# Sparse attention on one core: fp32r score parts, an unrolled unit sequence with the next group's preparation in it, and modulation sums split over two engines

## The reference, cut to what matters

```
mod  = silu(c) @ w_mod + b_mod            # 2048 x 12288 weights, 100 MB
hmix = modulate(rms_norm(x), sh_a, sc_a)
proj = hmix @ w_in                        # columns for pooling, linear and sparse attention
x1   = x  + g_a * (concat(pool, gla, nsa) @ w_out)
y    = x1 + g_f * swiglu(modulate(rms_norm(x1), sh_f, sc_f))
```

```
q, k_slc, k_win: rms-normalised per head, times a gain
for each group g, each token t:
  s_c = q . k_cmp (31 compressed blocks)  - slope * distance -> softmax p_c -> o_c = p_c @ v_cmp
  s_s = q . k_slc (causal)                - slope * distance -> softmax     -> o_s
  s_w = q . k_win (causal, 512 window)    - slope * distance -> softmax     -> o_w
  o   = gate0 * o_c + gate1 * o_s + gate2 * o_w
```

## Time and profile before

| | us |
|---|---|
| median of 3 runs | 2662.19 (2658.03 to 2663.2) |
| span of the profiled execution (first to last instruction) | 2663.0 |
| PE / PEld busy | 2525.8 / 2041.4 |
| DVE / ACT / POOL busy | 898.4 / 789.2 / 997.9 |
| attention stage | about 679 to 959 of the span |

### The profile page before, as it was taken

How to read it: one execution, slowest core, us unless ns; L and a number is a source line. 1 busy time by engine, 2 the same in 40 slices (tenths; PEclk the granted TensorE clock), 3 DMA queues, 4 the chain that set the end, 5 groups by cost and what they waited for, 6 DMA issues and landing times.

```text
span 2663.0 us, 33971 instructions
## 1 busy us (share of the span) xinstructions
PE 2525.8 (95%) x11449; PEld 2041.4 (77%) x11449; DVE 898.4 (34%) x1487; ACT 789.2 (30%) x1490; POOL 997.9 (37%) x764
## 2 busy tenths in 40 slices
PE   4589999998799999989999999999999999999999
PEld 3577777876677777868888888888888888888887
DVE  4755332147666666676202020202010101010112
ACT  2023224231455542232222222222222222222221
POOL 0024334443200024435444444444444444444443
PEclk8579999998888899989999999999999999999999
DMA  8742122346311246645222222222222222222223
GB/s 305 252 135 80 64 95 81 111 160 235 107 64 63 79 153 210 224 154 184 95 95 95 95 91 91 94 95 95 95 95 94 91 92 93 95 95 95 95 94 111
DMA packets 86204, 315.74 MB, mean 119 GB/s; under 512 B 9584, under 2 KB 10240, under 8 KB 84736
## 3 DMA queue, kind: packets, MB, share of 16 engines
q1 hardware_dynamic: 84240, 303.31, 34.5%
q10 hardware_dynamic: 1904, 11.62, 1.2%
HBM read 310.69 MB, written 4.19 MB: 118 GB/s over the span
## 4 chain that ended last, share of the span: by engine, by line
PE 57%; issue 30%; POOL 10%; DVE 1%; POOLq 0%; ACT 0%; DMA 0%; DVEq 0%; ACTq 0%; SPq 0%
PE ps L363 54%; POOL wlo L315 10%; PE ps L669 1%; PE ps L640 1%; PE ps L658 1%; DVE macc L1108 0%; PE ps L647 0%; POOLq L314 0%; DMA modw<-in_mstream 0%; DVE biasT L1383 0%; PE ps L675 0%; ACT pbuf L986 0%; PE ps L625 0%; POOL kn L337 0%; DVE sbuf L1431 0%
## 5 line engine op out<-in xcount | busy, mean ns | idle before, releaser
L315 POOL TENSOR_TENSOR wlo<-raw,whi 128x512 fp32r<-128x512 f32 x728 | 960.3, 1320 | 1506.7 <-ACT whi L797 1227.3
L797 ACT ACTIVATE whi<-raw 128x512 fp32r<-128x512 f32 x612 | 386.6, 632 | 1242.8 <-PE ps L363 1237.2
L363 PE MATMUL ps<-hfH,whi 128*128 128x512 f32 x1408 | 560.1, 398 | 12.3 <-DVE hfL L1489 11.5
L363 PE MATMUL ps<-hfL,whi 128*128 128x512 f32 x1408 | 559.0, 397 | 0.0
L363 PE MATMUL ps<-hfH,wlo 128*128 128x512 f32 x1408 | 559.0, 397 | 0.0
L363 PEld LDWEIGHTS ps<-hfH,whi 128*128 128x128 f32 x1408 | 266.2, 189 | 76.2 <-issue 12.3
L363 PEld LDWEIGHTS ps<-hfH,wlo 128*128 128x128 f32 x1408 | 266.2, 189 | 62.3
L363 PEld LDWEIGHTS ps<-hfL,whi 128*128 128x128 f32 x1408 | 266.4, 189 | 61.6
L1517 DVE SCALAR_TENSOR_TENSOR x1T<-ps,modc,x1T 128x512 f32<-128x512 f32 x176 | 132.2, 751 | 456.3 <-PE ps L363 456.3
L363 PE MATMUL ps<-huH,whi 128*128 128x512 f32 x704 | 279.2, 397 | 0.5 <-DVE huL L1500 0.5
L363 PE MATMUL ps<-huH,wlo 128*128 128x512 f32 x704 | 279.1, 396 | 0.0
(11 more groups left out here) (242 smaller groups left out, 2709.3 us busy)
## 6 DMA issues: line engine op xcount, KB each, us to landing
raw<-in_wstream SPq DMA_DIRECT2D x370, 512.0 KB, 3.4
modw<-in_mstream SPq DMA_DIRECT2D x192, 512.0 KB, 4.6
xT<-in_xt SPq DMA_DIRECT2D x4, 1024.0 KB, 8.5
w1s<-in_w ACTq DMA_DIRECT2D x2, 2048.0 KB, 8.3
x1T<-in_xt ACTq DMA_DIRECT2D x4, 1024.0 KB, 8.6
out_y<-x1T SPq DMA_DIRECT2D x16, 256.0 KB, 2.0
cmpb<-in_cmp_tab ACTq DMA_DIRECT2D x1, 1024.0 KB, 7.3
ptab<-in_tabs ACTq DMA_DIRECT2D x1, 768.0 KB, 4.4
```

Of the source, the lines that this page charges most:

```text
L315: nc.gpsimd.tensor_tensor(wlo[:, s, :], raw[:, r, :], whi[:, s, :].bitcast(F32), ALU.subtract).then_inc(unit_ready, 1)
L363: ins = nc.tensor.matmul(acc, lhs, rhs, start=first and n == 0, stop=last and n == 2)
L797: A(whi[:, k % SPLIT, :], raw[:, k % 8, :], ACT.Copy).then_inc(unit_hi, 1)
```

## The change

Scores. The group's queries are laid out once for each head with both halves of the partitions the same (`qn` now holds each query twice), and after the transposes ACT writes the fp32r high part of all 128 partitions while DVE overwrites partitions 64 to 127 with the low part: `qs` holds [q_high; q_low]. Keys: `kA` holds [k_high; k_high], `kB` holds [k_low; 0]. Scores are two fp32r matmuls, qs x kA and qs x kB, in place of one fp32 matmul. The compressed scores do the same with `kcA`, `kcB`. Score banks: two instead of three, so the scores of unit n wait for the minimum of unit n-2; the third bank takes the preparation.

Unrolling. The 128 units of all groups are one straight sequence. The preparation of group g+1 is six steps (keys of two branches, queries of four tiles), done after units 9, 12, 15, 18, 21 and 24 of group g: PE transposes, ACT copies the high part, and DVE subtracts one unit later. The bias tables of the next group are made at units 26 to 31, each after the last use of the row. The combine of tile 3 stands at unit 2 of the next group.

Queries of groups 2 and 3. Their squares are summed at units 3 and 5 of group 0, ACT takes the root at unit 14, DVE the inverse at 15, and POOL multiplies.

Modulation, q 12 to 15. DVE takes the even blocks of rows into `macc` at units 8, 11, ... 29, and POOL the odd ones into `macc2` with a multiply and an add; a piece's slot is free when both are done with it. PE sums both at unit 6 of the next group. Ahead of the output stage's weight pieces SP now waits until DVE has done all 32.

In the diff `scores` is PE's, `odd_rows` and the list behind it POOL's, `prep_high` ACT's (behind the saving of the unit); the rest is DVE's.

```diff
-                    nc.tensor.matmul(ps[:, n % 3, 0:w], qT[:, r // 2, t * P:(t + 1) * P],
-                                     kz[:, 2 * b + r % 2, 0:w], start=True, stop=True).then_inc(s_psum, 1)
+                q_ = qs[g % 2][:, t, r * P:(r + 1) * P]
+                nc.tensor.matmul(ps[:, n % 2, 0:w], q_, kA[g % 2][:, b, 0:w], start=True, stop=False)
+                nc.tensor.matmul(ps[:, n % 2, 0:w], q_, kB[g % 2][:, b, 0:w], start=False,
+                                 stop=True).then_inc(s_psum, 1)
...
+            def odd_rows(q):
+                pool.wait_ge(mod_summed, q)
+                for d in range(8):
+                    pool.wait_ge(mod_landed[d % 4], 32 * q + 16 * (d // 4 + 1))
+                    src = modw[:, d % 4, U:2 * U]
+                    scal = cact[:, 2 * d + 1:2 * d + 2].to_broadcast([P, U])
+                    if d == 0:
+                        TT(macc2[:, :], src, scal, ALU.mult).then_inc(mod_used, 1)
+                    else:
+                        own(TT(src, src, scal, ALU.mult))
+                        TT(macc2[:, :], macc2[:, :], src, ALU.add).then_inc(mod_used, 1)
+                    pool.wait_ge(mod_used, 8 * q + d + 1)
...
+            gains(1)
+            odd_rows(12)
+            pool.wait_ge(rq_ready, 1)
...
+            TT(q_j, q_j, rq[:, 1, :].unsqueeze(2).to_broadcast([P, 2 * T * R, DH]), ALU.mult).then_inc(qk_norm, 1)
+            pool.wait_ge(qk_norm, 3)
+            gains(2)
+            odd_rows(13)
+            gains(3)
+            odd_rows(14)
+            odd_rows(15)
...
+            def prep_high(g, step):
+                act.wait_ge(n_tr, 6 * g + step + 1)
...
+                dst = kA[g % 2][:, step, :] if step < 2 else qs[g % 2][:, step - 2, :]
+                A(dst, ps[:, prep_bank(g, step), :], ACT.Copy).then_inc(n_hi, 1)
...
+            def prep_low(g, step):
...
+                dve.wait_ge(n_hi, 6 * g + step + 1)
+                if step < 2:
+                    V.tensor_tensor(kB[g % 2][0:64, step, :], ps[0:64, bank, :],
+                                    kA[g % 2][0:64, step, :].bitcast(F32), ALU.subtract).then_inc(n_lo, 1)
...
+            def even_rows(q, d):
...
+                dve.wait_ge(mod_landed[d % 4], 32 * q + 16 * (d // 4 + 1))
...
+                    dve.wait_ge(mod_even, 8 * q + d)
+                    ins = V.scalar_tensor_tensor(out=macc[:, :], in0=src, scalar=scal, in1=macc[:, :],
+                                                 op0=ALU.mult, op1=ALU.add)
+                ins.then_inc(mod_even, 1)
...
+                if n % 8 == 2 and n >= 8:
+                    combine(T * g + t - 1)
+                if g + 1 < G and m >= 26 and (b == 0 or r == R - 1):
+                    dve.wait_ge(s_saved, n + b)
+                    bias(g + 1, r - 1 + b)
+                if g and m == MOD_SUM_AT + 1:
+                    finish_mod(g + 11, 2)
+                if g + 1 < G and m - 1 in PREP_AT:
+                    prep_low(g + 1, PREP_AT.index(m - 1))
+                if m in MOD_AT:
+                    even_rows(g + 12, MOD_AT.index(m))
```

More of the change, by code:

```diff
@@ new lines, in cmp_scores @@
+            def cmp_scores(tile):
+                g, t = tile // T, tile % T
+                if tile:
+                    pe.wait_ge(o_saved, tile + 4)
+                else:
+                    pe.wait_ge(kc_lo, 1)
+                key = slice(g * NCMP, (g + 1) * NCMP)
+                for r in range(R):
+                    q_ = qs[g % 2][:, t, r * P:(r + 1) * P]
+                    dst = ps[:, 7, r * NCMP:(r + 1) * NCMP]
+                    nc.tensor.matmul(dst, q_, kcA[:, key], start=True, stop=False)
+                    ins = nc.tensor.matmul(dst, q_, kcB[:, key], start=False, stop=True)
+                ins.then_inc(cs_psum, 1)
@@ new lines, in transposes, with values @@
+            def transposes(n):
+                t = units[n][1]
+                pe.wait_ge(p_ready, n + 1)
+                if n >= 2:
+                    pe.wait_ge(pt_saved, n - 1)
+                for c in range(t + 1):
+                    ins = nc.tensor.transpose(ps[:, 3 + n % 2, c * P:(c + 1) * P], pbuf[:, n % 2, c * P:(c + 1) * P],
+                                              ident[:, :])
+                ins.then_inc(pt_psum, 1)
+            def values(n):
+                g, t, r, b = units[n]
+                pe.wait_ge(pt_saved, n + 1)
+                if r == 0 and b == 0 and T * g + t >= 2:
+                    pe.wait_ge(o_saved, T * g + t + 3)
+                for c in range(t + 1):
+                    v_b = kv_tok[b][:, c, G * DH + g * DH:G * DH + (g + 1) * DH]
+                    ins = nc.tensor.matmul(ps[:, 5 + t % 2, b * 256 + r * DH:b * 256 + (r + 1) * DH],
+                                           pT[:, n % 2, c * P:(c + 1) * P], v_b, start=c == 0, stop=c == t)
+                ins.then_inc(pv_done, 1)
@@ new lines, in cmp_values @@
+            def cmp_values(tile):
+                pe.wait_ge(cpt_saved, tile + 1)
+                nc.tensor.matmul(ps[:, 7, 256:512], pcT[:, :], bd[:, tile // T, :], start=True,
+                                 stop=True).then_inc(cpv_done, 1)
+            pe.wait_ge(c_saved, 1)
+            for step in range(6):
+                prep(0, step)
+            scores(0)
+            scores(1)
+            for n in range(NU):
+                g, t, r, b = units[n]
+                m = n % 32
+                if n + 2 < NU:
+                    scores(n + 2)
+                if n % 8 == 4:
+                    cmp_scores(T * g + t)
+                if n % 8 == 7:
+                    pe.wait_ge(cp_ready, T * g + t + 1)
+                    nc.tensor.transpose(ps[:, 7, P:2 * P], pc[:, :], ident[:, :]).then_inc(cpt_psum, 1)
+                transposes(n)
+                if n >= 1:
+                    values(n - 1)
+                if n % 8 == 0 and n:
+                    cmp_values(T * g + t - 1)
+                if g and m == MOD_SUM_AT:
+                    pe.wait_ge(n_lo, 6 * g + 6)
+                    sum_columns(g + 11, 2, halves=True)
+                if g + 1 < G and m in PREP_AT:
+                    prep(g + 1, PREP_AT.index(m))
@@ L1445, in _ @@
-            own.leave(G)
+            for t in range(T):
+                dve.wait_ge(proj_saved, 28 + t + 1)
+                q_t = q_tok[:, 0:2, t, :]
+                ins = V.tensor_tensor(nsq[:, :].rearrange("p (g t c) -> p g t c", g=2, t=T)[:, :, t, :], q_t, q_t, ALU.mult)
+            own(ins)
+            own(V.tensor_reduce(rq[:, 0, :], nsq[:, :].rearrange("p (n d) -> p n d", d=DH), AX.X, ALU.add))
+            V.tensor_scalar(rq[:, 0, :], rq[:, 0, :], 1.0 / DH, EPS, ALU.mult, ALU.add).then_inc(qk_var, 1)
```

427 lines of the change are left out of this document (208 added, 219 removed).

## The result

The changed kernel takes 2706.64 us (median of 4 runs, 2705.20 to 2716.58), the kernel before 2660.68 beside it (4 runs, 2658.03 to 2663.20): ratio 1.0178, 95% interval 1.0166 to 1.0190. It is 46 us slower, where 11 us faster was forecast, and outside the range.

What follows compares the result with a forecast made beforehand. TensorE, busy 95%, bounds the kernel; in the attention stage tile 3 is PE's, tile 1 DVE's, tile 2 both's. Stage 30 us plus start 3 us saved, less 22 contention, gives 11 us less: 2651 us, range 2622 to 2674.

Steps and rivals of the forecast that it cites:

- the waits of the preparation: DVE subtractions waiting for ACT's copies at units 13, 16, 19, 25: 1.9 us each, some 7 us in each of three groups.
- the modulation sums: Half of DVE's 16 steps a group go to idle POOL; DVE gives back 11.4 us a group.
- the granted clock: PE's clock, noted as 0.75 in the seam and 0.55 in the first tile; no term in the sum.
- the column sums: PE's modulation column sums leave the seam for unit 6 of the next group; no price named.
- contention: POOL and DVE share a port: 144 DVE instructions x 0.25 = 36 us in the stage, taken as 22.
- rival 2: An alternative outcome whose text is missing from the prediction as given; chance 0.19.
- its own sum: PE's work in the attention stage: 45 to 50 us a group, setting the end if all prep waits are hidden.
- the seam: 10.0 us stretch after a group's tiles: nothing remains in groups 0 to 2, 4 us at the end of group 3.
- the 9.9 us of tile 0: DVE's chain in a group's first token tile after the change, forecast at 9.9 us.
- The scores in fp32r: Two passes take 0.46 us for 0.91 at 512 columns; a tile 3 unit on PE becomes 1.74 us.
- Rival 3: POOL's lock repeatedly delays dependent DVE chains in combines and compressed softmaxes: 2668 to 2687, nearer 2674; chance 0.19 shared with another rival.
- the softest term: Prep waits as the least certain term: saving about 50 us if all hidden, 23 if each costs half as much again.

## Why the prediction was wrong, step by step

Two terms of the sum were mis-sized, the waits of the preparation and the modulation sums, and two prices stood in it at nothing, the granted clock and the column sums.

**The waits of the preparation: mis-sized by more than a factor of two.** The text took 1.9 us at four of six steps, some 7 us in each of three groups, 21 in all, and named half as much again as the worst. The trace has 48.5 us, 18 of the 24 subtractions being in groups 1 to 3. The mean of the 16 recorded waits is 3.0 us. The sum of 1.9 us followed the copy through ACT alone (exponential, saving of a unit, copy). It left out PE's order. The copy also waits for the prep transposes, and these stand on PE behind the unit's own transposes and the values of the unit before: from 751.76 values, 752.48 the compressed branch's values, 752.97 the prep, copy from 753.61 to 754.21, and DVE idle since 750.93. A combine or compressed softmax that was to hide two of the six did not hide them either. One unit later the waits are 9.8 us, and with the sums back on DVE 4.1. In time, the later place of the subtractions was worth 20.5 us by itself and 35 once the sums were back on DVE.

**The modulation sums: the wrong sign.** 11.4 us a group were to come back from DVE, against 22 us of contention in all. In the kernel before the split alone costs 15 us, and with POOL's operations cut to 8 columns nothing. In the changed kernel the eight sums put back on DVE are 8 x 0.70 = 5.6 us a group in the forecast's terms, 22 in four groups, and take away its 22 of contention: no change. It gave 21 us. So by the medians the gain counted was not there and the contention was. Why DVE's time was worth so little is not shown; one reading is that others waited for DVE less often than the 1.06 us of a step suggests: even in tile 1, which the text gave to DVE, it was busy 9.7 of 12.7 us.

**The granted clock: not in the forecast's sum at all.** It stood in rival 2 as something for tile 0. The rows show 0.67 to 0.85 in tiles 1 to 3 of group 1, where the earlier trace rows have 1.00. In the four tiles PE is busy 68.2 us, far from the 45 to 50 of its own sum in the forecast; each tile's busy time times its granted clock adds up to 52 (an estimate from these rows), so the work was forecast about right and the rate was not. In tile 3 of group 0 a gap of 4.05 us cost as much again behind it: the next three units take 10.8 us (762.20 to 772.99), and 6.7 in the run with idle products (762.58 to 769.28). The idle products show it by subtraction, 12 us gained by adding some 11 us of work.

**The column sums in tile 0: not in the sum either.** The text took them out of the seam and named no price for them (the 9.9 us of tile 0 is 1.3 more than the 8.6 of its named terms, and doesn't say for what). PE now does eight products at unit 6, from 786.55 to 790.07 in group 1, and DVE's reading of them and the next minimum stand behind:

```profile
790.19 0.16 DVE L1243 TENSOR_TENSOR modc<-ps,vec 128x4 f32<-128x4 f32 x1 [3.27 <-PE ps L491]
```

That is 10.0 us of idle DVE in three groups, and 4.7 with the sums back on DVE, where four products are left. No run moves them alone, so what they cost in time is open.

**Contention: near in size, wrong in what it was set against.** Forecast 22 us, measured 14 by small operations (and 14 of 15 in the kernel before). POOL was busy 86 us in the stage, where 105 were forecast. The additions of the combine went from 0.43 us to 0.69 and 0.64 in the mean, as forecast (0.2 to 0.3 more). At the start it was worse than forecast: four bias tables beside POOL's gains and first rows take 8.10 us in the changed kernel, 4.69 in the kernel before and 3.19 in the run with all sums on DVE and late low parts. The first minimum is 0.85 us later than before instead of 3 us earlier.

**The scores in fp32r: right in rate, small in effect.** Two passes are 0.54 us instead of 0.91, near the 0.46 forecast, and a unit of tile 3 at full clock is 1.80 us against 1.74. But of the 9.6 us that four tiles 3 were to save (4 x 2.4), the kernel before gives 5 in all.

**The seam: gone, but in part moved.** Tile 0 of group 1 takes 15.4 us, where it took 10.8 and was forecast at 9.9. Free of the preparation's work the kernel is 49.5 us faster; with the work kept, its low parts two units after the high ones and the sums back on DVE, 56 us.

The outcome lies beyond all rivals. Rival 3 had the sign, with 2674, but by the lock in chains, which is worth 14 us of 46. Nearest to the truth was the sentence that called the prep's waits the softest term; its bound was too narrow, as it was made from one engine's queue.

What remains open: why half the sums on DVE bring nothing in the median of the kernel before; how the last 22 us between small GpSimd rows and sums on DVE divide; what the column sums and the third bank cost in the changed order; and how the 46 us divide between waits, bursts and clock, since the clock falls behind a burst as well as where DVE waits.

## What to carry to other kernels

Where a new wait is placed in an engine's order, trace the awaited result back through every engine's queue, not only through its maker's, and put the waiting instruction a full round of the pipeline later: here one unit of distance was worth 20 us. Count what PE loses after it has run dry, too: here the work behind the gap ran at half rate. A wait just ahead of a gap need not be its cause: the waits were taken away here, and the gap stayed. Work moved to an idle engine isn't free where it shares the first engine's port; do that half of a change alone before joining it to another.

## What the runs showed of the hardware

Idle f32 products of 3.65 us before an expected gap kept the granted clock at 1.00 in the tile behind it (0.80 without them), and the kernel gained 12 us. Without them the clock came back at 772.0, after 9.8 us in which PE was never idle at 0.50 to 0.52; with the low parts one unit later PE was busy without a pause for 18.0 us (755.37 to 773.40) at 0.50.

A DVE addition of 0.43 us lasted 2.38 and 2.46 us beside POOL operations of 2.4 us, twice in a row: the second one met the second operation. With 128x8 operands in place of 128x512 (0.23 us for 1.10) on POOL the kernel with split sums was back at the time of the kernel before (2661.86 and 2661.83 us).
